# Cross-attention between products of two layers of Strassen-like pairs: casts moved, Exp's table loaded ahead, and the softmax scaling given to ScalarE

## What is computed

```
def cross_attn(c_q, mk, mv):
    q = c_q.reshape(*lead, C_HEADS, C_HD)
    s = jnp.einsum('bthd,bmhd->bhtm', q, mk).astype(jnp.float32) * (C_HD ** -0.5)
    p = jax.nn.softmax(s, axis=-1).astype(mv.dtype)
    return jnp.einsum('bhtm,bmhd->bthd', p, mv).reshape(*lead, C_WIDTH)
...
    out_c = cross_attn(c_q, mk, mv) * jax.nn.silu(c_z)
...
    gates = jax.nn.sigmoid(gate_logits + b_gate).reshape(*lead, N_BRANCH, D_MODEL)
    proj = jnp.einsum('btic,icd->btid', br, w_branch)
    return jnp.sum(gates * proj, axis=-2) @ w_out
```

## Time and profile before

| | us |
|---|---|
| median of 3 runs (856.86 to 858.16) | 856.88 |
| profiled execution, its time | 858.03 |
| profiled execution, its span | 856.1 |
| TensorE busy | 834.7 (97%) |
| VectorE busy | 484.8 (57%) |
| ScalarE busy | 400.1 (47%) |
| GpSimd busy | 67.7 (8%) |

### The profile page before, as it was taken

One profiled execution on the slowest core, in us unless ns is written; L12 is line 12 of the kernel. 1 busy time (PEld: TensorE's weight loads), 2 busy tenths in 40 slices (PEclk: granted clock), 3 DMA queues, 4 the chain that ended last, 5 costly groups with the idle time before them and its releaser, 6 DMA issues.

```text
span 856.1 us, 16402 instructions
## 1 busy us (share of the span) xinstructions
PE 834.7 (97%) x6827; PEld 811.4 (95%) x6827; DVE 484.8 (57%) x828; ACT 400.1 (47%) x687; POOL 67.7 (8%) x122
## 2 busy tenths in 40 slices
PE   8999999999999999999999999999998899999997
PEld 7999999999999999999999999999888888899995
DVE  6537542735464385313327797546777888745534
ACT  7544446348766543422232253333346767643424
POOL 1001000000000222001012111001120000000000
PEclk9999999999999999999999999999999999999999
DMA  9334743331322759524267754316544342262402
GB/s 306 95 95 144 256 146 100 99 101 52 121 75 87 258 187 346 183 99 140 84 222 270 277 195 151 100 51 245 197 159 137 99 131 67 69 245 70 136 1 101
DMA packets 87206, 126.22 MB, mean 147 GB/s; under 512 B 3114, under 2 KB 73816, under 8 KB 87136
## 3 DMA queue, kind: packets, MB, share of 16 engines
q1 hardware_dynamic: 73328, 76.58, 27.7%
q0 software_dynamic: 13712, 48.57, 15.8%
q10 hardware_dynamic: 96, 0.06, 0.0%
HBM read 112.98 MB, written 12.22 MB: 146 GB/s over the span
## 4 chain that ended last, share of the span: by engine, by line
PE 89%; DVE 5%; ACT 3%; issue 1%; DMA 1%; SPq 0%; ACTq 0%; DVEq 0%
PE mm L1311 54%; PE mm L1268 5%; PE mm L1283 5%; PE mm L1348 3%; PE mm L1257 3%; PE mm L1601 2%; PE mm L1683 2%; PE p L1242 1%; PE p L1244 1%; PE p L1243 1%; PE mm L1622 1%; PE mm L1621 1%; PE mm L1620 1%; PE p L1560 1%; PE p L1530 1%
## 5 line engine op out<-in xcount | busy, mean ns | idle before, releaser
L1817 DVE TENSOR_TENSOR w_lo<-raw,w_hi 128x1024 fp32r<-128x1024 f32 x114 | 138.8, 1221 | 84.9 <-ACT w_hi L631 83.5
L1311 PE MATMUL mm<-h_lo,w_hi 128*128 128x260 f32 (+1 forms) x832 | 170.2, 286 | 0.0
L1311 PE MATMUL mm<-h_hi,w_hi 128*128 128x260 f32 (+1 forms) x832 | 167.5, 283 | 0.0
L1311 PE MATMUL mm<-h_hi,w_lo 128*128 128x260 f32 (+1 forms) x832 | 167.2, 283 | 0.0
L1311 PEld LDWEIGHTS mm<-h_lo,w_hi 128*128 128x128 f32 x832 | 128.1, 189 | 2.5 <-issue 2.4
L1311 PEld LDWEIGHTS mm<-h_hi,w_lo 128*128 128x128 f32 x832 | 128.3, 188 | 0.0
L1311 PEld LDWEIGHTS mm<-h_hi,w_hi 128*128 128x128 f32 x832 | 128.2, 188 | 0.0
L631 ACT ACTIVATE w_hi<-raw 128x1024 fp32r<-128x1024 f32 x114 | 118.9, 1052 | 11.6 <-DMA raw<-in_w_mem_kv_dram 6.2
L1311 PE MATMUL mm<-x_lo,w_hi 128*128 128x260 f32 (+1 forms) x448 | 96.3, 285 | 0.0
L1311 PE MATMUL mm<-x_hi,w_hi 128*128 128x260 f32 (+1 forms) x448 | 95.4, 283 | 0.0
L1311 PE MATMUL mm<-x_hi,w_lo 128*128 128x260 f32 (+1 forms) x448 | 95.3, 283 | 0.0
(11 more groups left out here) (445 smaller groups left out, 1767.8 us busy)
## 6 DMA issues: line engine op xcount, KB each, us to landing
raw<-in_w_in_dram SPq DMA_DIRECT2D x43, 1024.0 KB, 5.5
raw<-in_w_branch_dram SPq DMA_DIRECT2D x12, 1024.0 KB, 5.1
raw<-in_w_mem_kv_dram SPq DMA_DIRECT2D x8, 1024.0 KB, 5.9
gate<-in_cache_mem_k_dram POOLq DMA_DIRECT2D x16, 512.0 KB, 6.2
tok<-in_cache_mem_v_dram POOLq DMA_DIRECT2D x14, 512.0 KB, 5.4
tok<-in_state_gla_dram POOLq DMA_DIRECT2D x8, 512.0 KB, 7.1
out_dram<-tok POOLq DMA_DIRECT2D x8, 512.0 KB, 7.2
work<-scr_q POOLq DMA_DIRECT2D x8, 512.0 KB, 4.8
```

The lines of the kernel that those rows point to most:

```text
L1311: ins = MM(mm[:, j % 2, a, 0:c1 - c0], wp[:, j, k, :], xp[:, k, c0:c1], start=(k == 0 and wp is w_hi and xp is xl), stop=(k == KT - 1 and ...
L1817: V.tensor_tensor(w_lo[:, j], raw[:, j // 2, :, (j % 2) * P:(j % 2 + 1) * P], f32(w_hi[:, j]), ALU.subtract).then_inc(split_done, 1)
```

## The change

It has six parts. (1) `att_soft` only inverts the sums; `att_exp` waits for that and scales the probabilities with four ACT.Copy instructions, with the inverse as scale per partition. (2) In each even pair an exponential of one column stands ahead of `pair_keep`, so that Exp's table is loaded there. (3) The casts of the next head, high and low, stand in step 2 rather than 3: on ScalarE ahead of `att_out`, on VectorE between the product with the gate and the low part of the result. (4) At the start of pair 0 the casts of head 0 stand ahead of T3's, on both engines. (5) The transposes go by rows of tokens and wait for one quarter of the probabilities at a time. (6) The counts of the semaphore anmx are doubled for part 1.

```
@@ act hooks
-                    if step == 3 and h < CH - 1:
-                        att_hi(h + 1)
                     if step == 1:
                         att_p(h)
                     if step == 2:
+                        if h < CH - 1:
+                            att_hi(h + 1)
                         att_out(h)
@@ act pair_keep
+                if q % 2 == 0:
+                    A(table, eps_col, ACT.Exp)
                 wait_product(act, "P6", q)
@@ act pairs
                     pair_copy(0)
+                    att_hi(0)
                     t_hi(3)
-                    att_hi(0)
                     last_hi(0)
@@ act att_exp
-                act.wait_ge(sem("anmx"), h + 1)
+                act.wait_ge(sem("anmx"), 2 * h + 1)
...
+                act.wait_ge(sem("anmx"), 2 * h + 2)
+                for n in range(NT):
+                    A(prob[:, n, :], prob[:, n, :], ACT.Copy, scale=rden[:, n:n + 1]).then_inc(sem("ap_ready"), 1)
@@ pe hooks
-                        pe.wait_ge(sem("ap_ready"), NT * (h + 1))
...
-                        for m in range(MT):
-                            for n in range(NT):
+                        for n in range(NT):
+                            pe.wait_ge(sem("ap_ready"), NT * h + n + 1)
+                            for m in range(MT):
@@ dve pairs
                 if q == 0:
+                    att_lo(0)
                     t_lo(3)
-                    att_lo(0)
@@ dve hooks
-                    if step == 3 and h < CH - 1:
-                        att_lo(h + 1)
...
                         V.tensor_tensor(tc, p45[:, :, :], tc, ALU.mult).then_inc(sem("oc_full"), 1)
+                        if h < CH - 1:
+                            att_lo(h + 1)
@@ dve att_soft
-                link(V.reciprocal(rden, den))
-                for n in range(NT):
-                    V.tensor_scalar(prob[:, n, :], prob[:, n, :], rden[:, n:n + 1], None, ALU.mult).then_inc(sem("ap_ready"), 1)
+                V.reciprocal(rden, den).then_inc(sem("anmx"), 1)
```

## The result

| | before | after |
|---|---|---|
| median of 4 runs each, us | 856.87 | 866.73 |
| lowest to highest | 856.86 to 858.16 | 865.37 to 869.71 |
| ratio, 95% interval | | 1.0104 [1.0082, 1.0125] |

What follows compares the result with a forecast made beforehand. It took TensorE, busy 834.7 of 856.1 us, as the bound, so only its waits could be won. The terms -0.1 + 0.4 + 1.3 + 1.8 + 0.2 gave +3.6 us, a median of 860.5, range 857.2 to 862.8.

Steps and rivals of the forecast that it cites:

- PV does not wait: Rival: ScalarE has room for the copies and the scores' waits shrink; 4.0 us less, 852.9; chance 0.12.
- the copies are cheap: Rival: the four scaled copies on ScalarE take 1.14 us, so about no change, 857.4 to 858.6; chance 0.18.
- A: From pair 0's start to the start of head 1's scores: -0.1 us, with 0.45 lost to slow clock.
- B: From the start of head 1's scores to the start of head 2's: +0.4 us, 29.85 against 29.48.
- C: From the start of head 2's scores to the start of head 3's: +1.3 us, 31.5 against 30.17.
- D: Head 3, from its scores on: no scores follow to give PV's delay back; +1.8 us, 16.7 against 14.89.
- 0.2 for P4: Small waits at P4, added to the sum: some 0.2 us.
- the clock: Rival: slow spell behind head 0's waits could reach P3, P6 and PV(0); up to +2 more, 862.5; chance 0.10.

Runs made afterwards that it cites:

- filler run: Changed kernel plus 25 small useless multiplications on TensorE in three of its waits (head 0's transposes, behind them, P4(5)); 863.85 us, ratio 1.0069 to before.
- order-only kernel: Changed kernel with the scaling back on VectorE, all order changes, early table load and transposes by rows kept; 858.04 us, ratio 0.9995 to before.
- scaling-only kernel: Kernel before with only the scaling moved to ScalarE and the transposes by rows; 865.39 us, ratio 1.0079.
- third trace: Changed kernel unaltered, one more execution; 865.25 us, no wait near 103 us, pairs 129.54 us.
- early load alone: Kernel before with only Exp's table loaded ahead of the wait for P6; 854.57 us, ratio 0.9959.
- with the small copies: Kernel before with the early table load, plus four one-column ScalarE copies beside each load that nothing needs; 854.15 us, ratio 0.9961.
- with pT_hi ahead: Changed kernel with pT_hi and pT_lo moved on both engines ahead of the next pair's casts, four copies still on ScalarE; 863.26 us, ratio 1.0072.

## Why the prediction was right in sign and wrong in size

**The mechanism held in the main.** PV waits for pT_lo in heads 1 to 3, 1.19 against "about 1.4"; P4(1) waits 0.9 (0.8), P4(5) 1.84 (1.9), the transposes 0.66 (0.5), head 0 3.27 (3.3); the scores wait for nothing in heads 1 to 3. Head 1's maximum starts 679.90 - 674.65 = 5.25 behind the scores (5.0). The copies are 16 of 493 ns (475). The rival "PV does not wait" is out, "the copies are cheap" too.

**Where the missing 4.5 us of the pairs lie** (8.1 measured, 3.6 forecast). The filler run has no slow clock and shows +4.8: A +0.07, B +0.86, C +1.69, D +2.17. The forecast without its 0.45 of slow clock had -0.55, +0.4, +1.3 and +1.8, and 0.2 for P4: 3.15. So 1.65 is not clock, and the other 2.85 (8.1 less 4.8 is 3.3, less the 0.45) is. Two slips in the prediction's sums, 4.2 for 0.9 + 3.4 and 1.8 for 3.6 - 1.72 - 0.2, change nothing.

**The 1.65 are small terms.** The four copies take 1.70 from SBUF, over both bounds (1.14 to 1.57): 0.13 a head. The maximum of head 1 starts 0.2 later than reckoned. With both, pT_hi comes 14.54 behind S(1) for 14.24 and PV 16.88 for 16.55; at head 0 P4 is 0.28 late. That is 0.3 a head, some 1.2 in all; where the rest lies was not followed up.

**Term A failed, and the step is the length of its slow stretch:** "4.2 us from the restart ... are over at 653, so only 1 us of P4 runs at half, 0.45 lost". The waits around it came as forecast: P4 starts 19.76 behind pair 0's start against 652.1 - 632.62 = 19.48. But the time at half clock, which was 3.4 us before, was 6.8 here. (A row over 5 us with a mean clock of 0.81 holds 1.9 us at half, one with 0.51 holds 4.9.) P4 and P3 took 4.71 us against 2.88 + 0.45 = 3.33, 18 of their 24 multiplications at half. That is 1.4 of the 1.95 missed in A. In the other traces of the changed kernel it was 16 (4.54 us), 22 (5.17) and all 24 (5.30), always in 6.8 us of slow clock, so where the stretch falls moves A by up to 0.8.

The forecast carried the length over from one trace with one shorter wait. The second wait of 1.5 is not needed for the double length: the order-only kernel has a single wait of 3.14 there, none at P4(0), and 6.9 us of slow clock (0.78 and 0.53 above); the scaling-only kernel has two waits, 1.69 and 1.81, and 3.4. In all nine traces that waited 3.1 us or more ahead of the transposes and had no fillers it was 6.8 or 6.9, in the six that waited 1.7 to 2.2 it was 3.4 five times and nothing once. What about the longer wait does it was not tried. The rival "the clock" had this, up to +2, with too small a chance.

**Term C failed in the same way at another place:** no slow clock was put behind P4(5)'s wait, because waits of 1.6 leave the clock at 1.00. Behind 1.84 it fell in two of the four traces of the changed kernel, at 1.5 us each time, and stayed up in the third and fourth. It fell in the order-only kernel too, so it doesn't take the copies. Without it C is +1.68 against +1.3.

**Ahead of the pairs** lie 1.4 to 3.6 us in three of the four traces of the changed kernel, from the wait near 103 us and, in the profiled execution, a slower start with a clock of 0.83 over 10 to 20. The forecast had nothing there. The third trace, 865.25 beside 858.23 for before in the same group, shows the cost without it: 7.0 us, of which 7.1 lie in the pairs. So of the 6.2 us between 866.73 and 860.5 3.5 to 4.5 are missed in the pairs, by the trace, and the rest is this.

The Trainium skill (ScalarE: Activation LUTs, Rules for kernel authors) gives multiplications to VectorE. Here that was right, 858.04 against 867.49, less for the 1.14 against 1.70 us, which are 2.2 us in four heads, than for where the copies stand: the pairs differ by 7.4.

## What to carry to other kernels

Before work goes to the less busy engine, read what stands behind it in that engine's queue: ScalarE at 47% had no gap just there, and 1.7 us of copies made PV 1.9 us later in each head. Where a change lengthens a wait of TensorE, price what runs behind it at both clock levels, and take the difference into the range. And take a change apart into its edits: here one edit of six was worth -3.5 us by itself, one cost 7, and the casts' move, placed three instructions later in VectorE's queue, no longer did harm. Where one trace of each kernel is compared, look first whether the clock fell in the same places: a stretch that fell in one and not in the other was worth 1.5 us here, as much as some of the edits.

## What the runs showed of the hardware

- Four scaled copies of 128x256 on ScalarE take 1.70 to 1.71 us from SBUF in the pairs of this kernel, 1.57 from PSUM in branch B.
- The length of a wait did not by itself decide the clock. Behind 1.84 us at P4(5) it fell or stayed in the same kernel; behind 1.95 at head 0 it fell (early load alone: 0.70 over 650 to 655) or stayed (with the small copies: 1.00); behind 2.53 at P4(5), with pT_hi ahead, it stayed:

```profile
729.37 0.35 PE L1353 MATMUL mm<-h_lo,w_hi 128*128 128x260 f32 x1 [2.53 <-DVE stage L1897]
...
730.00:735.00 5.00, 5.00 (x44) 5.00 (x43) 3.31 (x7) 3.27 (x7) 0.00 (x0) 1.00 0.00 0
```

- The time at half clock around head 0 was 3.4 us behind waits of 1.7 to 2.2 us (five of six traces) and 6.8 to 6.9 behind waits of 3.1 us or more (nine of nine).
- The 25 filler multiplications in waits gave back 3.1 us of clock in the pairs, against a trace in which it had fallen at both places.
- One execution of an unchanged program may differ from the next by 1.4 us in one wait near 103 us, where a weight block's DMA let ScalarE wait 2.85 us in one execution and not at all in another.
